# Differential heads first, the remaining projections between attention blocks, x parked in DRAM

## The reference, cut to what matters

```
for l in range(2):
    proj = rms_norm(x) @ w_in[l]                     # split into three kinds of heads
    o_mla  = mla_attention(h_mla, ...)               # 6 heads; needs q = norm(c_q) @ w_uq, k,v = norm(c_kv) @ w_ukv
    o_diff = diff_attention(h_diff, ...)             # 6 heads; softmax(map 0) - lam * softmax(map 1)
    o_ch   = chunk_attention(h_ch, ...)              # 4 heads; one map each, relative bias
    x = x + concat(norm(o_mla), norm(o_diff), norm(o_ch)) @ w_out[l]
    x = x + conv_ffn(rms_norm(x)) @ ...
```

## Time and profile before

| | |
|---|---|
| median of 3 runs | 2241.1 us (2235.74 to 2247.72) |
| the profiled execution | 2234.8 us, its span 2233.1 us |
| token stage, layer 0 and layer 1 | 106.3 to 140.5 us, 788.1 to 822.2 us |
| up stage | 140.5 to 162.7, 822.2 to 845.9 |
| attention stage | 162.7 to 255.1, 845.9 to 941.4 |
| PE busy over the span | 92% |

### The profile page before, as it was taken

One profiled execution on the slowest core, in us unless ns is written; L12 is line 12 of the kernel. 1 busy time (PEld: TensorE's weight loads), 2 busy tenths in 40 slices (PEclk: granted clock), 3 DMA queues, 4 the chain that ended last, 5 costly groups with the idle time before them and its releaser, 6 DMA issues.

```text
span 2233.1 us, 24957 instructions
## 1 busy us (share of the span) xinstructions
PE 2058.0 (92%) x8468; PEld 1328.9 (60%) x8469; DVE 1186.7 (53%) x1968; ACT 692.5 (31%) x1230; POOL 743.0 (33%) x1218
## 2 busy tenths in 40 slices
PE   7999889999998999988999999999998898898895
PEld 5865468888786874466888786455333445333332
DVE  6546766678546445667678744326881623111113
ACT  4328734334323317734334422130000501111010
POOL 0306766756201006766666400003660000111110
PEclk9999999999999999999999999999998998899898
DMA  4210122232223210122333223112231054799983
GB/s 172 85 41 1 39 94 104 104 113 98 87 95 119 95 50 1 39 75 86 109 116 114 75 91 108 57 58 106 110 123 57 26 219 163 310 422 423 424 328 153
DMA packets 44259, 284.19 MB, mean 127 GB/s; under 512 B 8394, under 2 KB 8650, under 8 KB 21632
## 3 DMA queue, kind: packets, MB, share of 16 engines
q1 hardware_dynamic: 34272, 254.35, 30.3%
q0 software_dynamic: 9024, 19.08, 2.2%
q10 hardware_dynamic: 864, 9.44, 1.0%
HBM read 272.68 MB, written 23.60 MB: 133 GB/s over the span
## 4 chain that ended last, share of the span: by engine, by line
PE 79%; DVE 8%; DMA 6%; ACT 3%; POOL 2%; issue 1%; SPq 0%; DVEq 0%; POOLq 0%; ACTq 0%
PE bank L813 11%; PE bank L815 10%; PE bank L814 10%; PE bank L1063 5%; DMA experts<-in_experts 5%; PE bank L1236 3%; PE bank L997 3%; PE bank L999 3%; PE bank L998 3%; PE bank L1033 2%; PE bank L1168 2%; PE bank L933 2%; PE bank L904 2%; PE bank L920 2%; PE bank L1264 1%
## 5 line engine op out<-in xcount | busy, mean ns | idle before, releaser
L813 PE MATMUL bank<-h_high,w_high 128*128 128x512 f32 x1056 | 418.6, 396 | 38.8 <-ACT h_high L1600 13.1
L814 PE MATMUL bank<-h_low,w_high 128*128 128x512 f32 x1056 | 415.6, 394 | 0.0
L815 PE MATMUL bank<-h_high,w_low 128*128 128x512 f32 x1056 | 415.5, 393 | 0.0
L1468 ACT ACTIVATE w_high<-extra 128x2048 fp32r<-128x2048 f32 (+1 forms) x104 | 180.5, 1736 | 349.7 <-DVE w_low L1871 349.6
L1868 DVE TENSOR_SCALAR extra<-ring 128x2048 int32<-128x2048 int32 (+1 forms) x104 | 117.3, 1128 | 264.6 <-PE bank L815 138.2
L813 PEld LDWEIGHTS bank<-h_high,w_high 128*128 128x128 f32 x1056 | 201.4, 191 | 91.7 <-issue 27.4
L815 PEld LDWEIGHTS bank<-h_high,w_low 128*128 128x128 f32 x1056 | 201.0, 190 | 42.8
L814 PEld LDWEIGHTS bank<-h_low,w_high 128*128 128x128 f32 x1056 | 201.5, 191 | 41.3
L1871 DVE TENSOR_TENSOR w_low<-ring,extra 128x2048 fp32r<-128x2048 f32 (+1 forms) x104 | 217.8, 2094 | 3.6
L1236 PE MATMUL bank<-experts,rstd 128*64 128x512 f32 x432 | 124.7, 645 | 23.3 <-DMA experts<-in_experts 13.9
L998 PE MATMUL bank<-act_low,w_high 128*128 128x512 f32 x352 | 139.2, 396 | 0.0
(11 more groups left out here) (438 smaller groups left out, 3770.5 us busy)
## 6 DMA issues: line engine op xcount, KB each, us to landing
experts<-in_experts SPq DMA_DIRECT2D x29, 2048.0 KB, 25.8
ring<-in_w_ffn_in SPq DMA_DIRECT2D x44, 1024.0 KB, 4.8
experts<-in_experts SPq DMA_DIRECT2D x29, 1024.0 KB, 26.1
ring<-in_w_ffn_out SPq DMA_DIRECT2D x32, 704.0 KB, 4.1
ring<-in_w_feature SPq DMA_DIRECT2D x14, 1024.0 KB, 4.8
last_slot<-in_experts SPq DMA_DIRECT2D x5, 2048.0 KB, 30.5
ring<-in_w_rest SPq DMA_DIRECT2D x9, 1024.0 KB, 4.9
ring<-in_w_out SPq DMA_DIRECT2D x8, 1024.0 KB, 4.9
```

The source lines that it names most:

```text
L813: pe.matmul(dst, high[:, at], h_high[:, k, :], start=k == 0, stop=False)
L814: pe.matmul(dst, high[:, at], h_low[:, k, :], start=False, stop=False)
L815: return pe.matmul(dst, low[:, at], h_high[:, k, :], start=False, stop=k == KD - 1)
L1468: act.activation(w_high[par_][:, 0:words], w_part[par_][:, 0:words], ACT.Copy).then_inc(w_split, 1)
```

## The change

What it does:

- The order of heads becomes differential (blocks 0 to 23), chunk (24 to 39), MLA (40 to 63). The outputs go to other tiles of h (`TILE_OF_PAIR`), and the sums over them are taken in the new order.
- The token tiles and the uq, uk and uv tiles leave their stages and stand between attention steps: one token tile ahead of step 0 and behind each of steps 0 to 10; uq of head 0 behind step 13, uk behind 15, uq of head 1 behind 17 and so on in steps of two to uk of head 5 behind 35; uv behind 37, 39, 41 and 43 (`BETWEEN`).
- Token tiles use banks 5 and 6 in turn, all small tiles bank 6 alone; value matmuls use bank 5 alone. So each small tile waits until the one ahead of it is copied out.
- DVE ropes a uq tile, and ACT copies a uq or uk tile (`up_copy`), ahead of the next block's softmax steps.
- `PBUF` goes from 12 to 14 buffers, which lie in other places; `pt` of even pairs lies in x. So x is written to DRAM at the start of layer 1 (2 MB; in layer 0 the input itself is used) and read back when the second to last pair's value matmuls are done. w_out's blocks can be loaded as soon as the ring has room.
- The relative bias is loaded behind the token tiles; POOL's power tables start once the last turn is done.

```diff
+TILE_OF_PAIR = (3, 4, 5, 6, 7, 0, 1, 2)
-PBUF = EXTRA_PROBS + 2
+PBUF = 14
+SMALL = [(name, h) for h in range(MLA_H) for name in ("uq", "uk")] + [("uv", tc) for tc in range(NQ)]
+BETWEEN = {n - 1: ("token", n // NQ, n % NQ) for n in range(TOKEN_BLOCKS * NQ)}
+BETWEEN.update({13 + 2 * n: name for n, name in enumerate(SMALL)})
 def attention_order():
-    order = []
+    order = [BETWEEN[-1]]
...
         if LAG <= t < NPB + LAG:
             order.append(("turn", t - LAG))
+        if t in BETWEEN:
+            order.append(BETWEEN[t])
...
-        pt = [ring[n].rearrange("p (c t) -> p c t", c=NQ) for n in (1, 2)]
+        pt = [x[:, NQ * n:NQ * (n + 1), :] for n in range(2)]
...
+                    sp.wait_ge(x_added, l * (2 * KD))
+                    sp.dma_start(x_d, x[:]).then_inc(x_parked, 16)
...
+                sp.wait_ge(pe_done, done(l, "heads", PAIRS - 2, NQ - 1))
+                sp.dma_start(x[:], x_d if l else a["x"]).then_inc(x_home, 16)
...
+                def up_tile(name, n):
+                    if name == "uq":
+                        w = weights(l, BLOCK_MLA)
+                        pe.wait_ge(token_out, l * (4 * NQ) + TOKEN_BLOCKS * NQ)
+                        pe.wait_ge(mla_normed, l * 3 + 3)
+                        pe.wait_ge(uq_out, l * (2 * MLA_H) + 2 * n)
...
+                    elif name == "uk":
+                        w = weights(l, BLOCK_MLA + 1)
+                        pe.wait_ge(uq_out, l * (2 * MLA_H) + 2 * n + 1)
+                        pe.wait_ge(roped, l * (MLA_H + 2) + (n + 3))
...
                 for u, (kind, hd, m, i) in enumerate(MAPS):
                     nk = (i + 1) * P
+                    t = PBLOCK_OF[u]
+                    if u == PBLOCKS[t][3][0] and BETWEEN.get(t - 1, ("",))[0] in ("uq", "uk"):
+                        up_copy(*BETWEEN[t - 1])
                     act.wait_ge(maxed, l * NMAPS + (u + 1))
                     act.activation(probs[u % PBUF][:, 0:nk], probs[u % PBUF][:, 0:nk], ACT.Exp, bias=stat[:, 0, u:u + 1],
...
                 for t, (kind, _, _, maps) in enumerate(PBLOCKS):
+                    name, n, *rest = BETWEEN.get(t - 1, ("", 0))
+                    if name in ("uq", "uv"):
+                        up_evac(name, n)
                     for u in maps:
                         biased_minimum(u)
+                    if name == "token":
+                        token_evac(n, *rest)
```

More of the change, by code:

```diff
@@ L686, in _ @@
                 load(l, BLOCK_MLA + 1, a["w_ukv"][l])
-                for n in range(BLOCKS_OUT):
+                sp.wait_ge(pe_done, done(l, "token", TOKEN_BLOCKS - 1, NQ - 1))
+                sp.dma_start(rel[:], a["rel"][l]).then_inc(rel_in, 16)
+                for n in range(RING):
+                    load(l, BLOCK_OUT + n, a["w_out"][l * BLOCKS_OUT + n])
+                sp.wait_ge(pe_done, done(l, "heads", PAIRS - 2, NQ - 1))
+                sp.dma_start(x[:], x_d if l else a["x"]).then_inc(x_home, 16)
+                for n in range(RING, BLOCKS_OUT):
                     load(l, BLOCK_OUT + n, a["w_out"][l * BLOCKS_OUT + n])
@@ L842, in _, with token_tile @@
                 pe.wait_ge(mla_squares, l * 3 + 3)
-                finish(pe.matmul(bank[5][:], c("ones"), sq3[:, 2, :], start=True, stop=True), "sum_kv", 0)
-                for b in range(TOKEN_BLOCKS):
+                pe.wait_ge(feature_out, l * 14 + 12)
+                finish(pe.matmul(bank[3][:], c("ones"), sq3[:, 2, :], start=True, stop=True), "sum_kv", 0)
+                def token_tile(b, tc):
                     n = FEATURE_BLOCKS + b
-                    pe.wait_ge(w_split, l * SPLITS + (n + 1))
@@ L864, in _ @@
-                w = weights(l, BLOCK_MLA)
-                pe.wait_ge(mla_normed, l * 3 + 2)
-                for hd in range(MLA_H):
-                    if hd < 4:
-                        pe.wait_ge(token_out, l * (4 * NQ) + (8 + hd + 1))
-                    else:
-                        pe.wait_ge(uq_out, l * (2 * MLA_H) + (hd - 3))
-                    for k in range(2):
-                        ins = pe.matmul(bank[hd % 4][:], w[:, (k * MLA_H + hd) * P:(k * MLA_H + hd + 1) * P], cqkv[:, k, :],
-                                        start=k == 0, stop=k == 1)
-                    finish(ins, "uq", hd)
@@ L875, in _ @@
[L875 to L884 removed]
+                    t = b * NQ + tc
@@ new lines, in token_tile @@
+                    tok = slice(tc * P, (tc + 1) * P)
+                    if tc == 0:
+                        pe.wait_ge(w_split, l * SPLITS + (n + 1))
+                    if t >= 2:
+                        pe.wait_ge(token_out, l * (4 * NQ) + (t - 1))
+                    dst = bank[5 + t % 2][:, 0:nw]
+                    for k in range(KD):
+                        at = slice(k * nw, (k + 1) * nw)
+                        pe.matmul(dst, h_high[:, k, tok], w_high[n % 2][:, at], start=k == 0, stop=False)
+                        pe.matmul(dst, h_low[:, k, tok], w_high[n % 2][:, at], start=False, stop=False)
+                        ins = pe.matmul(dst, h_high[:, k, tok], w_low[n % RING][:, at], start=False, stop=k == KD - 1)
@@ L910, in _ @@
                         finish(ins, "scores", n)
+                    elif step == "token":
+                        token_tile(*name[1:])
+                    elif step in ("uq", "uk", "uv"):
+                        up_tile(*name)
                     elif step == "turn":
@@ L1530, in turn @@
                     pair = t // PAIR
+                    if t == 0 and l:
+                        act.wait_ge(x_parked, 16 * l)
+                    if t == PAIR:
+                        act.wait_ge(pe_done, done(l, "token", TOKEN_BLOCKS - 1, NQ - 1))
                     if t % PAIR == 0 and pair >= 2:
```

238 lines of the change are left out of this document (129 added, 109 removed).

## The result

The changed kernel takes a median of 2213.1 us (2212.2 to 2214.9, four runs); the kernel before, on the same chip, 2238.8 (2235.7 to 2247.7, four runs). The ratio is 0.9878, 95% interval 0.9850 to 0.9906: faster by 1.2%, 26 us. The forecast was 2239 and its range began at 2221, so both were wrong, on the fast side.

The account below looks back on a forecast made before the run. PE, busy 92% of the span, was taken to bound the kernel, with its pauses and clock. Per layer -8.9 + 9.6 + 0.8 = +1.5, two layers +3.0, clock -4.5: -1.5 from 2241.1, forecast 2239, range 2221 to 2253.

Parts of the forecast that it names:

- the sum of -1.5: Whole kernel: +1.5 us per layer, +3.0 for two layers, and -4.5 for the clock, together -1.5 us.
- Removed pauses: Up stage and attention: PE's pauses filled by tiles between blocks, 8.9 us per layer removed, bounds 3.5 to 9.5.
- Added copies: Small tiles sharing bank 6: PE waits for ACT's copy of the tile before, 9.6 us per layer, bounds 0 to 13.
- tile shapes: Inserted uk tiles: PE loses time when the tile shape changes, 0.8 us per layer, bounds 0 to 2.5.
- the first rival: Small tiles: ACT's copies hide behind pauses PE would have anyway, so the 9.6 falls away, giving 2220; chance 0.26.
- The clock: Differential stretch, mostly layer 1: dense work takes back 9 of 20.4 us at 0.50, 4.5 us gained, bounds -10 to 8.
- the second rival: Step 12 to layer end: low clock spreads with short pauses, 9.8 us slower, giving 2254; chance 0.11.
- Ropes ahead of the minima: Small-tile steps on DVE: ropes of 2.2 us covered by PE's work, cost nothing; uncovered 13 us per layer.
- x parked: Layer 1's write of x and the 2 MB fetch near attention's end: forecast to cost nothing, both ways.
- The slower side's: Step 12 to layer end: more low clock from short pauses, 9.8 us slower, giving 2254; chance 0.11.
- The last sentence: Steps 0 to 11: the forecast would be wrong altogether if the token tiles found pauses of their own; no size given.

Follow-up runs that it names:

- the eighth run: Changed kernel with the twelve token tiles all ahead of the attention blocks, as in the kernel before; median 2237.9 us, ratio 1.0006 to the kernel before.
- the first run: Changed kernel with ACT copying each uq or uk tile at the end of its step, ahead of the transposed block's copies; median 2199.4 us, ratio 0.9821.
- the last run: Changed kernel with ACT copying all of a uq tile at its step's end and ropes behind minima of single-map blocks; median 2196.8 us, ratio 0.9816.
- the seventh run: Changed kernel with the uq ropes behind the minima of their step instead of ahead of them; median 2235.3 us, ratio 0.9979.
- the paced run: Changed kernel with each differential score matmul waiting for one minimum more, as with one score bank less; median 2281.2 us, ratio 1.0178.
- run 31: Not a run's number: the words are "the paced run 31 and 48", where 31 is that run's us at 0.50 clock; median 2281.2 us.

## Why the prediction was wrong

**The step that failed** is its first sentence on the change, part by part: "PE's matmuls are the same in number and size, so only pauses and clock can move." Number and size were the same, and their busy time fell by 9.8 and 10.9 us a layer, since how far they overlap depends on when their banks come free. Shown: the same scores take 32 us a layer in one row group (some 29 without the low clock), 20 or 21 in the kernel before, 10 in the changed one. With this term at 9.8 twice, the sum of -1.5 would have been -21.1, and the forecast 2220. The trace of before had the sign of it: weight loads of L904 waiting 0.18 us for DVE again and again inside a stretch that PE's row gives as one busy block. The earlier trace rows were read for PE's idle time alone, and the list of waits named DVE's hold on L904 with only 1.0 us, because it counts idle PE.

**Why the banks come free in time**: the token tiles between the blocks, 2.85 us each, let DVE finish its four minima before PE is back. Taking them away (the eighth run) costs 25 us and all of the gain; some 4 of the 25 are that run's own, the wait for the normalisation, and by the estimate of 0.33 some 13 are the low clock, which leaves some 8 for the overlap and the pauses. That the low clock came from the lost fillers is likely by its place and not shown. Fourteen buffers do part of the same job (0.9% in the kernel before, nothing measurable beside the tiles). The order of the heads was not tried apart; with it kept and the token tiles ahead the time is that of the kernel before. The forecast took the fillers for a cover of pauses, and so valued them at the pauses.

**Removed pauses** (8.9 us a layer forecast): steps 0 to 11 have no pause over 0.25 us, as said, and the up stage's are gone. **Added copies** (9.6): counted between matmuls, 1.05, 1.20, 1.31, 1.46, 1.05, 1.20, 0.93, 0.98, 0.25, 0.94 and 0.93 us in front of eleven small tiles, 11.3 us, beside the 0.85 at the end, which the forecast let stand. Mechanism and steps right, size 1.7 too small: 1.0 of it in steps 15 to 25, whose six waits are 7.3 us and not 6.2, 0.4 in steps 27 to 35, where the chunk steps hide less than was taken, and 0.2 at uv(0). The other three uv tiles wait for nothing, as forecast. Net idle grew by 2.2 and 2.7 us as shown; the forecast had 0.7, and 0.8 more for tile shapes (its own count, 12 changes at some 0.1, is 1.2). That these waits are on the path, which the first rival doubted, is shown by the first run: 13.7 us less with nearly all of them gone.

**The clock** (-4.5): the 3.4 and 17.0 us at 0.50 are all gone. Layer 1 took 4.5 us longer than layer 0 before, for 13.6 us more of low clock (0.33 us each), and now takes as long; for all 20.4 us that is some 6.7 us, a part of which lies inside the scores' terms. That the size is near was in part luck, as two errors went against each other: all 20.4 us came back and not 9, at 0.33 us each and not 0.5. Its reason, dense work where the low windows were, fits the eighth run, in which the token tiles are gone from there and the clock is at 0.50 for 20.4 us a layer, but was not tried apart. That short pauses bring the low clock, as the second rival had it, isn't borne out, as the last section shows.

**Ropes ahead of the minima** at nothing: right for what they hold up, the score groups are near their shortest (10.20 us, 9.96 in the last run). But with the ropes behind the minima the time is 22 us longer, as the seventh run shows, 13 of it waits of the uk tiles and the rest mostly low clock; the prediction never priced the other place. The parts don't add up: taking back this one or the token tiles costs nearly all of the 26 us each time, so no part owns a share. **x parked**: stretch by stretch nothing in attention; 3 us are given back behind it, among the experts, in single profiles, and this was not tried apart.

**The rivals.** The first one gave 2220 and was nearest, for the wrong reason: its copies weren't hidden. The slower side's, more low clock from more short pauses, went the other way. The last sentence says that the forecast would be wrong altogether if the token tiles found pauses of their own. They found none (PE is busy 42.48 of 42.60 us there), and it was wrong by a term that no rival named.

## What to carry to other kernels

Where small matmuls go to different row groups, compare the busy time of one group with that of the same group when all its banks are free (2.55 and 1.14 us here), then look at the weight loads: a PE that is shown busy all the time can be waiting inside such a group, and its waiting stands in no list of PE's idle time. Before a large change, try more buffers first: two gave 0.9% here. Filler between such groups helped in pauses and in overlap. And where two engines read one bank, let the faster one copy all of it, and place the other, which then reads the copy, where its engine has slack: ropes in four-map steps cost 10 us against the same ropes in single-map steps, the 10.2 us of low clock of that run included.

## What the runs showed of the hardware

- Four 32-row maps of 512 columns in four row groups take 0.98 us, in one 3.54 us, and released one by one 0.47 us apart 2.39 us; each instruction's own duration reads 480 ns on average in the two kernels that use four row groups, and has the same 270, 480 and 692 ns (least, median, most) in the groups shown for one row group.
- The low clock didn't follow the number of pauses. The changed kernel has ten of 0.9 to 1.5 us a layer and not one window at 0.50 in these stretches. The run in one row group has the same pauses, longer busy time, and 27 and 21 us at 0.50; the paced run 31 and 48; the run with its token tiles ahead 20.4 in each layer, right over the paced groups. What in these stretches brings it was not taken apart and stays open. The Trainium skill, "TensorE: Matmul & The Clock Gate", section "A second HAM failure mode: psum-queue depth-cycling", lays the swings to short pauses between groups; by the changed kernel's ten pauses the trace doesn't agree, and the clock gave back some 6.7 us where that rule would have had nothing.
